# Where a third block's split, a down product and the attention's reads stand in five engines' queues

## The reference

```python
# first block
h  = layer_norm(concat(meta, x))                      # 272 tokens
p  = h @ w_in + b_in                                  # columns for S5, q, k, v, gates
... # a state-space mixer, four mLSTM heads, two output products
h  = layer_norm(ALPHA * h + mix @ w_o)                # "n1"
ff = square(relu(h @ w_up + b_up)) @ w_down           # 32 tiles of 128 columns
h  = layer_norm(ALPHA * h + ff)                       # "n2"
# second block
q, k, v, z = split((rmsnorm(h) * (1 + sc1) + sh1) @ w_in_2)
attn = softmax(q @ k.T * scale) @ v                   # 8 heads of 64
tok  = gelu(z) halves, mixed over tokens              # the token branch
x = h + gt1 * (concat(rmsnorm(attn), rmsnorm(tok)) @ w_out)
y = rmsnorm(x) * (1 + sc2) + sh2                      # "r2"
z = conv3(y @ w_up_2)                                 # 2 x 22 tiles of 128 columns
x = x + gt2 * ((silu(z_a) * z_b) @ w_down_2)
out = rmsnorm(x)                                      # "out"
```

## Time and profile before

| what | us |
|---|---|
| median of three runs | 834.3 |
| lowest and highest of them | 833.6 and 839.08 |
| profiled execution | 836.29 |
| span of its trace | 834.5 |
| TensorE busy (matmuls) | 776.1 (93%) |
| VectorE busy | 574.0 (69%) |
| ScalarE busy | 472.3 (57%) |
| GpSimd busy | 135.3 (16%) |

### The profile page before, as it was taken

How to read it: one execution, slowest core, us unless ns; L and a number is a source line. 1 busy time by engine, 2 the same in 40 slices (tenths; PEclk the granted TensorE clock), 3 DMA queues, 4 the chain that set the end, 5 groups by cost and what they waited for, 6 DMA issues and landing times.

```text
span 834.5 us, 14481 instructions
## 1 busy us (share of the span) xinstructions
PE 776.1 (93%) x5365; PEld 705.9 (85%) x5365; DVE 574.0 (69%) x836; ACT 472.3 (57%) x768; POOL 135.3 (16%) x144
## 2 busy tenths in 40 slices
PE   3999999999999979999999997998777999999995
PEld 2899999888899859889898986997656999999994
DVE  7985678743677575666574748985457798966675
ACT  4975565456675464554545538557347555556554
POOL 3100000000124021233232210000000221233321
PEclk9999999999999989999999999999788999999998
DMA  7363333144355667788676751842033666565631
GB/s 271 98 198 136 127 102 125 53 120 159 101 178 176 216 212 245 240 306 318 238 292 252 263 191 50 313 175 95 26 101 103 207 232 216 177 203 176 200 128 51
DMA packets 45863, 147.49 MB, mean 177 GB/s; under 512 B 9308, under 2 KB 10076, under 8 KB 45808
## 3 DMA queue, kind: packets, MB, share of 16 engines
q1 hardware_dynamic: 44544, 144.88, 51.1%
q10 hardware_dynamic: 1264, 1.86, 0.7%
HBM read 144.59 MB, written 1.05 MB: 175 GB/s over the span
## 4 chain that ended last, share of the span: by engine, by line
PE 84%; DVE 5%; ACT 5%; issue 4%; POOL 1%; DMA 1%; ACTq 0%; DVEq 0%; SPq 0%; POOLq 0%
PE ps L755 28%; PE ps L491 20%; PE ps L705 19%; PE ps L719 1%; PE ps L1008 1%; PE ps L765 1%; PE ps L553 1%; PE ps L505 1%; PE ps L679 1%; PE ps L567 1%; PE ps L946 1%; PE ps L582 1%; DMA vtk<-in_x 1%; PE ps L913 1%; PE ps L620 1%
## 5 line engine op out<-in xcount | busy, mean ns | idle before, releaser
L1604 DVE TENSOR_TENSOR wl<-raw,wh 128x1024 fp32r<-128x1024 f32 x220 | 281.6, 1283 | 146.2 <-ACT wh L1082 145.2
L1082 ACT ACTIVATE wh<-raw 128x1024 fp32r<-128x1024 f32 x220 | 231.3, 1053 | 69.7 <-PE ps L705 54.7
L755 PE MATMUL ps<-xh,wh 128*128 128x256 f32 x672 | 191.7, 285 | 3.9 <-DVE taps L2227 2.5
L755 PE MATMUL ps<-xh,wl 128*128 128x256 f32 x672 | 189.6, 282 | 0.0
L755 PE MATMUL ps<-xl,wh 128*128 128x256 f32 x672 | 189.5, 282 | 0.0
L755 PEld LDWEIGHTS ps<-xh,wh 128*128 128x128 f32 x672 | 128.2, 191 | 7.4 <-DVE taps L2227 2.7
L755 PEld LDWEIGHTS ps<-xl,wh 128*128 128x128 f32 x672 | 128.2, 191 | 2.4 <-issue 0.2
L755 PEld LDWEIGHTS ps<-xh,wl 128*128 128x128 f32 x672 | 128.1, 191 | 0.0
L491 PE MATMUL ps<-xh,wh 128*128 128x256 f32 (+1 forms) x400 | 117.7, 294 | 2.0 <-POOL xl L2288 1.0
L491 PE MATMUL ps<-xh,wl 128*128 128x256 f32 (+1 forms) x400 | 113.9, 285 | 0.0
L491 PE MATMUL ps<-xl,wh 128*128 128x256 f32 (+1 forms) x400 | 113.8, 284 | 0.0
(11 more groups left out here) (408 smaller groups left out, 1297.3 us busy)
## 6 DMA issues: line engine op xcount, KB each, us to landing
raw<-in_w_stream SPq DMA_DIRECT2D x220, 512.0 KB, 3.5
ada_w<-in_w_ada SPq DMA_DIRECT2D x48, 512.0 KB, 5.0
vtk<-in_x SPq DMA_DIRECT2D x2, 512.0 KB, 4.5
out<-ob SPq DMA_DIRECT2D x4, 256.0 KB, 2.0
u<-uT SPq DMA_DIRECT2D x16, 34.0 KB, 2.5
eepp<-in_s_mats SPq DMA_DIRECT2D x1, 512.0 KB
bti<-btr SPq DMA_DIRECT2D x16, 32.0 KB, 2.4
ws<-in_w_s ACTq DMA_DIRECT2D x1, 512.0 KB, 3.9
```

Of the source, the lines that this page charges most:

```text
L755: mm = nc.tensor.matmul(ps[:, bank, 0:SEQ], w, x, start=(k == 0), stop=(k == 3 * KD - 1))
L1082: nc.scalar.activation(wh[:, b % RING], raw[:, b % RING], ACT.Identity).then_inc(hi_done, 1)
L1604: V.tensor_tensor(wl[:, b % RING], raw[:, b % RING], wh[:, b % RING].bitcast(F32), ALU.subtract).then_inc(lo_done, 1)
```

## The change

1. **Third block behind a norm.** `hi` of block B_F1 + 2, B_IN2 + 2 and B_F2 + 2 goes to ScalarE's list inside the norm (behind `normed(0, 1)`; in r2 behind `row_bias(1)`), `lo` to VectorE's list between the norm and the split.
2. **Down products.** In the first feed-forward the down product of tile j - 2 follows the up product of tile j, and the packing follows. In the second one only the end is reordered: up 20, up 21, down 19.
3. **Attention.** `exps` stand ahead of `probt_copy`, `att_hi` and `att_lo` behind both, and the read of banks 0 and 1 is cut in two: the scaled pieces are taken first in blocks 2 and 4, their sums are added behind the maxima.
4. **Input turns.** Four of the eight turns stand ahead of the first products, the others between these. `hi(3)`, `lo(2)` and `lo(3)` come earlier, and VectorE's small phases go between the tiles.

```diff
-            def first_blocks(b, banks, ready, first=META):
-                for n in range(2):
-                    pe.wait_ge(*lo_made(b + n))
+            def first_blocks(b, banks, ready, first=META, between=None):
                 for m in range(KD):
+                    if between:
+                        between(m)
                     pe.wait_ge(*ready(m))
                     a, z = xh[:, m, first:TOK], xl[:, m, first:TOK]
                     for n in range(2):
+                        if m == 0:
+                            pe.wait_ge(*lo_made(b + n))
...
-            for k in range(KD):
+            def turn_x(k):
                 if k >= 6:
                     pe.wait_ge(LN["hi"], k - 5)
                     pe.wait_ge(LN["h"], k - 5)
...
-            first_blocks(B_U, (0, 1), lambda k: (LN["lo"], k + 1), 0)
+            for k in range(4):
+                turn_x(k)
+            first_blocks(B_U, (0, 1), lambda k: (LN["lo"], k + 1), 0, lambda k: turn_x(k + 4) if k < 4 else None)
...
             def pair(j, i=0):
-                if j >= 2:
-                    block(B_F1 - 1 + 2 * j, up_bank(j), "f_relu", i * 8 + (j - 1), i * 16)
-                rows_down(B_F1 + 2 * j, j - 1, "f_lo", i * 8 + j, F1_BANKS, i * 16, first=(j == 1))
-            for j in range(1, LOOP1_PAIR - 1):
+                block(B_F1 - 2 + 2 * j, up_bank(j), "f_relu", i * 8 + (j - 1), i * 16)
+                rows_down(B_F1 - 1 + 2 * j, j - 2, "f_lo", i * 8 + (j - 1), F1_BANKS, i * 16, first=(j == 2))
+            for j in range(2, LOOP1_PAIR - 1):
                 pair(j)
...
-            block(B_F1 + 2 * KF - 3, up_bank(KF - 1), "f_relu", KF - 2)
+            block(B_IN2 - 4, up_bank(KF - 1), "f_relu", KF - 2)
+            rows_down(B_IN2 - 3, KF - 3, "f_lo", KF - 2, F1_BANKS)
...
-            for j in range(KF2 - 4, KF2 - 1):
+            for j in range(KF2 - 4, KF2 - 2):
                 triple(j)
-            up2(KF2 - 1)
+            up2(KF2 - 2)
+            up2(KF2 - 1, 0, NBLK - 5)
+            rows_down(NBLK - 3, KF2 - 3, "ff2_lo", KF2 - 2, F2_BANKS)
...
@@ scalar
             hi(2)
+            hi(3)
...
-                hi(b + AHEAD)
+                if b:
+                    hi(b + AHEAD)
                 evac(b)
...
                 normed(0, 0)
                 normed(0, 1)
+                hi(b)
                 root(1)
...
             split("n1", y, lambda m: col("ln1_g", m), lambda m: col("ln1_b", m))
-            hi(B_F1 - 1 + AHEAD)
...
             def pair(j, i=0):
-                b, t = B_F1 - 1 + 2 * j, i * 16
+                b, t = B_F1 - 2 + 2 * j, i * 16
...
-            hi(B_IN2 - 1 + AHEAD)
...
             for b in range(B_OUT2, B_F2):
                 n = b - B_OUT2
-                if n in (2, 3, 4, 5):
-                    att_hi(n - 2)
                 if b < B_F2 - 1:
                     hi(b + AHEAD)
+                if n < 3:
+                    exps(2 * n + 2)
+                    exps(2 * n + 3)
                 if n < 4:
                     probt_copy(2 * n)
                     probt_copy(2 * n + 1)
-                if n < 3:
-                    exps(2 * n + 2)
-                    exps(2 * n + 3)
                 if n == 0:
                     q_std(2)
+                if n in (2, 3, 4, 5):
+                    att_hi(n - 2)
...
                 row_squares(t, 0)
                 row_bias(t)
+                if t:
+                    hi(B_F2 - 1 + AHEAD)
                 row_squares(t, 1)
...
-            hi(B_F2 - 1 + AHEAD)
...
-            for q in range(KF2 - 4, KF2):
+            for q in range(KF2 - 4, KF2 - 1):
                 triple(q)
+            high2(KF2 - 2, 0)
+            centre_taps(KF2 - 1, 0, 0, NBLK - 5)
+            hi(NBLK - 1)
+            centre_taps(KF2 - 1, 0, 1, NBLK - 5)
+            silu2(KF2 - 1, 0)
             high2(KF2 - 1, 0)
@@ vector
             lo(0)
             lo(1)
-            ...                       # L1635 to L1644, and L1651 to L1667 behind the eight L1649
+            def phases(k):            # the same operations, in eight parts, one behind each L1649
+                ...
             for k in range(KD):
                 ...
+                phases(k)
+            lo(2)
+            lo(3)
...
             angles(0)
-            lo(2)
-            lo(3)
...
                 V.tensor_scalar(xn[:, 1, 0:512], ps[:, banks[1][0], :], tmv[:, 1, 0:1], tstd[:, 1, 0:1], ALU.subtract, ALU.mult)\
                     .then_inc(LN["norm"], 1)
+                lo(b)
...
-            lo(B_F1 - 1 + AHEAD)
...
-            lo(B_F1 + 2 * KF - 1 + AHEAD)
...
-            def out2(n, dh):
-                dve.wait_ge(blk_done, B_OUT2 + n + 1)
-                for t in range(NT):
-                    gated_part(t, t, t, 0, dh)
-                for t in range(NT):
-                    add_part(t, t, dh, False)
...
                 n = b - B_OUT2
-                if n in (2, 3, 4, 5):
-                    att_lo(n - 2)
+                if n in (2, 4):
+                    dve.wait_ge(blk_done, b)
+                    for t in range(NT):
+                        gated_part(t, t, t, 0, n // 2 - 1)
...
                 if n < 3:
                     maxima(2 * n + 2)
                     maxima(2 * n + 3)
+                if n in (2, 4):
+                    for t in range(NT):
+                        add_part(t, t, n // 2 - 1, False)
...
                 if 1 <= n < 5:
                     attended(n - 1)
-                if n == 2:
-                    out2(1, 0)
-                if n == 4:
-                    out2(3, 1)
+                if n in (2, 3, 4, 5):
+                    att_lo(n - 2)
...
+            lo(B_F2 - 1 + AHEAD)
             split("r2", tg_m, lambda m: gain[:, 1, m:m + 1], lambda m: mod[:, M_SH2 + m:M_SH2 + m + 1])
-            lo(B_F2 - 1 + AHEAD)
...
-            for j in range(KF2 - 4, KF2):
+            for j in range(KF2 - 4, KF2 - 1):
                 triple(j)
+            outer_taps(KF2 - 1, 0, 0)
+            lo(NBLK - 1)
+            outer_taps(KF2 - 1, 0, 1)
@@ packing
-    ffn1 = np.concatenate([up[:1], np.stack([up[1:], down[:-1]], 1).reshape(-1, P, D), down[-1:]])
+    ffn1 = np.concatenate([up[:2], np.stack([up[2:], down[:-2]], 1).reshape(-1, P, D), down[-2:]])
...
```

More of the change, by code:

```diff
@@ L1040, in _, with up2 @@
             turn_normed("r2", (ln("r2", "norm"), ln("r2", "norm", 2), ln("r2", "norm", 3), ln("r2", "norm_act")))
-            def up2(j, i=0):
+            def up2(j, i=0, b=None):
                 t = i * 12
-                b = B_F2 + 3 * j - 1
+                b = b or B_F2 + 3 * j - 1
                 block(b, 0, "ff2_ca", i * 4 + j, t)
@@ L1291, in _, with token_norm @@
                     nc.scalar.activation(std[:, 0:1], eps[:, 0:1], ACT.Sqrt)
-            def token_norm(tag, banks, eps_col):
+            def token_norm(tag, banks, eps_col, b):
                 def root(t):
@@ L1311, in _ @@
             y = res[:, :, META:TOK]
-            token_norm("n1", WO_BANKS, eps[:, 0:1])
+            token_norm("n1", WO_BANKS, eps[:, 0:1], B_F1 - 1 + AHEAD)
             def split(tag, dst, g_of, b_of):
@@ L1362, in _ @@
                     pair(LOOP1_PAIR + q, i)
-            token_norm("n2", F1_BANKS, eps[:, 1:2])
+            hi(B_IN2 - 2 + AHEAD)
+            token_norm("n2", F1_BANKS, eps[:, 1:2], B_IN2 - 1 + AHEAD)
             for m in range(KD):
@@ L1533, in _, with centre_taps @@
             split("r2", tg_m, lambda m: gain[:, 1, m:m + 1], lambda m: mod[:, M_SH2 + m:M_SH2 + m + 1])
-            hi(B_F2 - 1 + AHEAD)
             act.wait_ge(S["mixed"], QT)
             act.dma_start(g_row, A["g_final"][None, :].to_broadcast([P, D])).then_inc(S["mixing_landed"], 16)
-            def centre_taps(j, i, which):
+            def centre_taps(j, i, which, b=None):
                 dst, bank, off = ((ca, 0, 0), (cb, 1, KF2))[which]
-                b = B_F2 + (0 if j == 0 else 3 * j - 1) + which
+                b = (b or B_F2 + (0 if j == 0 else 3 * j - 1)) + which
                 act.wait_ge(blk_done, i * 12 + (b + 1))
@@ L1634, in _ @@
             lo(1)
-            dve.wait_ge(S["half_done"], 1)
-            step(V.tensor_tensor(sv[:, 0:2], span("lam_re lam_im").rearrange("p (a s) -> p a s", a=2),
-                                 dt[:, None, :].to_broadcast([P, 2, NS5]), ALU.mult))
-            dve.sem_inc(S["phase_done"], 1)
-            V.tensor_tensor(sigk, sigma[:, None, :].to_broadcast([P, STEP, NS5]), power, ALU.mult).then_inc(dve_step, 1)
-            step.n += 1
-            step(V.tensor_scalar(near, theta, 1.0 / TWO_PI, ROUND, ALU.mult, ALU.add))
@@ L1642, in _ @@
-            step(V.tensor_scalar(near, near, ROUND, None, ALU.subtract))
-            for part in (PI_A, PI_B, PI_C):
-                step(V.scalar_tensor_tensor(theta, near, -part, theta, ALU.mult, ALU.add))
+            def phases(k):
+                if k == 0:
+                    dve.wait_ge(S["half_done"], 1)
```

(29 more changed lines are left out.)

23 lines of the change are left out of this document (3 added, 20 removed).

## The result

The changed kernel took 814.51 us in the median of four runs (812.86 to 815.72), the kernel before 835.09 (833.6 to 839.08): ratio 0.9745, interval 0.9705 to 0.9785, or -20.6 us. The forecast was 814.0. The profiled execution took 813.64 us with a span of 811.8, which is 22.7 less than the span before.

The account below looks back on a forecast made before the run. TensorE was taken to bound the kernel, busy 776.1 of 834.5 us, leaving its waits and the half clock behind them. Terms summed to -20.2, taking the profiled 836.3 to 816.1 and the median to 814; range 808.5 to 820.5.

Parts of the forecast that it names:

- Attention, -15.5: Attention: waits of 2.4, 4.6 and 3.0 us go with the half clock behind them, 15.5 us saved.
- what I named as late next: Attention: the weighing of the third pair asks for `att_lo` of the first, with 0.7 us of slack.
- Rivals 1 and 4: Attention: 1, only its waits gained, 9 saved, 820.5, 13%; 4, clock stays at 1.2 GHz, +6.5, 836, 2%.
- First feed-forward, -4.8: First feed-forward: early `hi` and `lo` let tile 2's up product cover the 3.2 us wait, half clock goes too; 4.8 saved.
- Rival 3: First norm: gaps around the second turn grow, the clock falls, `first_blocks` products cost 2.6 us more; 816.7, 10%.
- Second norm, -0.1: Second norm: insertion costs 0.45 us and takes 1.05 us from ScalarE behind the norm; nearly cancelling, 0.1 us saved.
- r2, -0.8, up to -1.8 more: Third norm: TensorE's 2.5 us wait for taps falls to 1.7; 1.8 us more if the clock stays full.
- the prediction's rule, half clock after every wait of 2.4 us or more: TensorE: after such a wait the clock is about 0.50 (1.2 GHz), so a removed wait counts nearly twice.
- Tail, -1.5: Second feed-forward's end: a down product covers the 1.5 us wait for GpSimd's low part of tile 21; 1.5 us saved.
- Start, +2.5: Start: the eighth tile turns about 3.0 us later, delaying ScalarE's list and block 0's evacuation; 2.5 us lost.
- VectorE's phases cost the same in either place: Start: moving VectorE's phases between the tiles was taken to change nothing in their cost.
- Rival 5: Start: turns among the products keep half rate longer, all 48 products at 0.22 us; +3.3, 817.5, 3%.

Follow-up runs that it names:

- turns first: The changed kernel with TensorE's eight input turns in one run again, the rest of the changed start kept; 815.4 us.
- start undone: The changed kernel with the whole start as before (turns, `hi(3)`, `lo(2)` and VectorE's phases); 813.59 us.
- start undone, relu no wait: The changed kernel with the start of before and no TensorE wait for the first relu ahead of the product of tile 2; 811.09 us.
- down two behind: The kernel before with only the first feed-forward's down products two behind, the third block's `hi` and `lo` left behind the norm's split; 830.64 us.

## Why the prediction was right, step by step

**Attention, -15.5.** The whole of stage E gave -17.5 in the profiles. Of it 1.3 us is no gain: before, the clock was at half at 564 us, ahead of everything that the lists move, and in the kernels "turns first" and "start undone" it is again (93.36 and 93.34 against 92.07). -16.2 stands against -15.5. The working held at each point: exponentials done at 579.14, 0.26 us before T (0.2 forecast); the pieces read at 579.44; the fourth product's pieces ready at 593.36 for a product at 593.83, 0.5 us of slack (0.3); and what I named as late next had what I gave it:

```profile
585.90 0.48 DVE L2097 SCALAR_TENSOR_TENSOR ml<-ps,cols,mh 128x256 fp32r<-128x256 f32 x1 [1.47 <-ACT mh L1440]
```

It ends at 586.38, the weighing that asks for it starts at 587.11: 0.7 us. The 0.6 us that I took off for handovers was not needed. Rivals 1 and 4 did not come: no stretch from T to the last row is under 1.00.

**First feed-forward, -4.8.** Stage C gives -3.9 in the profiled pair and -4.2 between the middles of either kind (247.6 and 243.4). The size holds, half of its reason does not. I made the early `hi` and `lo` the condition; the order alone brings 4.6, and the insertion costs 0.3 us, which I had priced at 0.65, and buys nothing here. The residual wait that I put down to GpSimd, 0.3 us, is 0.9 us for the relu: it stands on ScalarE behind the last `xh`, the issue of its four loads and a `hi`, a queue that I had not counted. Rival 3, the fall of the clock there, has been seen in two of seven profiles with the insertion ("start undone" and "start undone, relu no wait", 0.50 in the first norm's blocks).

**Second norm, -0.1.** -0.6 in stage D in six of seven profiles, less the 0.2 us of the longer gap in C: -0.4. I had the delay at 0.45 and so the two as nearly equal.

**r2, -0.8, up to -1.8 more.** -1.0 in stage F, and the clock behind the taps stays up: the wait of 1.34 us left it at 1.00 in all seven profiles that have it, that of 2.45 us lowered it in four of six. That is the 1.6 us between 192.8 and 191.22 in stage G. So the prediction's rule, half clock after every wait of 2.4 us or more, is too strong: it holds in most profiles only. I had left the clock's part in the range; five of the seven profiles with the insertion give the saving of stage F back, 0.9 us, so that F and G together bring 0.1 to 2.6.

**Tail, -1.5.** -1.7, and +1.7 when undone.

**Start, +2.5.** +3.0 in the profiled pair, and 2.2 or 4.2 in the four profiles of the changed start against the middle of the old ones, 46.2. The two values differ by the wait of block 2, 2.35 or 2.78 us, and by how long the clock then stays at 0.50, about 3.4 or 6 us. The mechanism is the one forecast: `hi` of tile 7 at 22.45 (22.5), the evacuation at 28.41 (28.6), block 2 at 28.93.

```profile
22.45 0.58 ACT L1102 ACTIVATE xh<-ps,cols 128x272 fp32r<-128x272 f32 x1 [0.70 <-PE ps L528]
...
28.41 0.47 ACT L1173 ACTIVATE uT<-ps,cols 128x272 f32<-128x272 f32 x1
...
28.93 0.39 PE L491 MATMUL ps<-xh,wh 128*128 128x272 f32 x1 [2.35 <-ACT uT L1173]
```

What I missed is the half clock behind the wait that I had forecast myself, 0.58 at 30 us: I applied "2.4 us lowers it" to waits that go and not to the one that comes. "VectorE's phases cost the same in either place" was wrong for VectorE (0.17 against 0.75 us a time) and right in effect, since TensorE hardly waits for them. Rival 5 and its rule did not decide: with the turns among the products, some 9 and 14 products stood 0.22 us apart in the two profiles of the changed kernel, with the turns first 7 in "before", 17 in "start undone, relu no wait" and 20 in "turns first". Full rate came 7.2 to 9.4 us behind the first turn with the turns among the products, in five profiles, and 8.2 to 11.2 us behind it with the turns first, in eight. That is not longer at half rate. Its price was a little low as well: a slow product costs 0.10 us more, not 0.09.

That the sum came out at -20.6 for -20.2 is luck in part, because what the terms missed is of both signs: attention, second norm and tail were better by 0.7, 0.3 and 0.2, the first feed-forward worse by 0.6, the start between 0.3 better and 1.7 worse, and r2 between 1.8 better and 0.7 worse. The two profiled executions alone are 22.7 us apart.

## What to carry to other kernels

Where three engines feed TensorE in turn, write down for each wait what stands ahead of its releaser in that engine's list, and move the work nobody waits for behind it; then fix the lists together, since half of the reorder left its own wait (4.2 and 11.6 us apart, 17.4 together). Price a wait that your change brings as you price one that it removes, with the clock behind it. And when one execution spreads by as much as an edit is worth, cut the span at matmuls that all kernels share: a stage that no edit touches shows how much of a difference is the clock.

## What was not expected of the hardware

- The same wait gives different clocks from one execution to the next. Behind 2.6 us at 210 us the granted clock stayed at 1.00 in two of thirteen profiles, and in the others stage B was 1.6 or 2.9 us longer. In the kernel "down two behind" the clock was at 0.50 for the whole way between two waits of the old attention, where before it came back:

```profile
580.30:592.60 12.30, 7.71 (x34) 6.57 (x34) 3.86 (x10) 4.33 (x11) 0.00 (x0) 0.50 0.00 0
```

- A small VectorE operation on SBUF that meets a GpSimd one of 0.77 us takes up to 0.75 us in place of 0.17, while one that reads PSUM keeps its 0.56 (VectorE's L1649 at 16.99 in "before", beside a `xl`).
- Even 0.46 us of waiting can stand ahead of a lower clock: behind the wait for `ada_acc` at 384 us it was 1.00 in two profiles and 0.66 in a third.
- In the first products of a run the granted clock reads 1.00 while they are 0.22 us apart; 2 to 5 us later they are 0.125 apart, with no other clock in the rows. How many are slow differs between profiles of one start (7 to 18 in seven profiles of the old one); the Trainium skill ("TensorE: Matmul & The Clock Gate", Part 1) says of such a count that it is "run-variable", and the trace agrees.
